# Norms inside the attention sweeps, cut in three: squares, then sums and root, then the scaling, each a unit later

## The reference, cut to what matters

```python
def rmsnorm(x, gain):
    xf = x.astype(jnp.float32)
    xf = xf * lax.rsqrt(jnp.mean(xf * xf, axis=-1, keepdims=True) + EPS)
    return xf.astype(x.dtype) * gain

def diff_mixer(q, k, v, qk_g, lam_p, o_g, lam_init):
    q = rmsnorm(q.reshape(B, S, DIFF_HEADS, 2, DIFF_QK), qk_g[0])
    k = rmsnorm(k.reshape(B, S, DIFF_HEADS, 2, DIFF_QK), qk_g[1])
    ...
    o = rmsnorm(o, o_g) * (1.0 - lam_init)

def swa_mixer(q, k, v, qk_g, sinks):
    q = rmsnorm(q.reshape(B, S, SWA_KV_HEADS, G, HEAD_DIM), qk_g[0])
    k = rmsnorm(k.reshape(B, S, SWA_KV_HEADS, HEAD_DIM), qk_g[1])
```

## Time and profile before

| | |
|---|---|
| median of 3 runs | 2279.16 us (2278.46 to 2280.85) |
| the profiled execution: its own time | 2280.71 us |
| its span in the profile | 2278.9 us |
| TensorE matmuls busy | 2146.6 us, 94% |
| VectorE busy | 1486.5 us, 65% |
| ScalarE busy | 1009.7 us, 44% |
| mean granted clock of TensorE | 0.983 |

### The profile page before, as it was taken

One profiled execution on the slowest core, in us unless ns is written; L12 is line 12 of the kernel. 1 busy time (PEld: TensorE's weight loads), 2 busy tenths in 40 slices (PEclk: granted clock), 3 DMA queues, 4 the chain that ended last, 5 costly groups with the idle time before them and its releaser, 6 DMA issues.

```text
span 2278.9 us, 32746 instructions
## 1 busy us (share of the span) xinstructions
PE 2146.6 (94%) x12051; PEld 1714.9 (75%) x12051; DVE 1486.5 (65%) x2695; ACT 1009.7 (44%) x1867; POOL 377.5 (17%) x346
## 2 busy tenths in 40 slices
PE   7999999999899998999999999999998989999996
PEld 4897788777677786777579878887866878777774
DVE  4637776654667876777656486766265678377775
ACT  4523334543465335555434233345344643345552
POOL 2002200000000341344300121000000014124441
PEclk9999999999999999999999999999999999999998
DMA  9322333331225675776542223423222266546753
GB/s 309 93 86 61 94 101 93 103 92 51 80 78 175 243 245 226 284 250 247 190 153 85 76 79 93 130 79 93 79 61 79 79 226 241 201 167 247 256 211 119
DMA packets 196573, 333.71 MB, mean 146 GB/s; under 512 B 30528, under 2 KB 153280, under 8 KB 180416
## 3 DMA queue, kind: packets, MB, share of 16 engines
q1 hardware_dynamic: 169184, 305.33, 39.6%
q0 software_dynamic: 19296, 19.98, 2.8%
q10 hardware_dynamic: 7936, 6.30, 0.8%
HBM read 352.48 MB, written 51.38 MB: 177 GB/s over the span
## 4 chain that ended last, share of the span: by engine, by line
PE 73%; DVE 13%; ACT 6%; issue 3%; DMA 3%; POOL 0%; SPq 0%; POOLq 0%; ACTq 0%; DVEq 0%
PE ps L874 68%; PE ps L872 5%; DVE spare L2077 2%; DVE ring_rounded L2095 2%; ACT WH_rounded L1587 2%; DVE nmax L2323 1%; DVE ssq L2262 1%; DMA SQKV<-gate_logits 1%; DMA DVt<-gate_logits 1%; DVE ps L2320 1%; DMA Y<-y_rows 1%; DVE DQK L2264 0%; DVE SC L2693 0%; ACT SC L1723 0%; POOL M L3035 0%
## 5 line engine op out<-in xcount | busy, mean ns | idle before, releaser
L874 PE MATMUL ps<-X_rounded,WH_rounded 128*128 128x512 f32 x768 | 343.8, 448 | 20.9 <-ACT CM L1635 6.5
L2095 DVE TENSOR_TENSOR ring_rounded<-ring,WH_rounded 128x512 fp32r<-128x512 f32 (+2 forms) x190 | 234.9, 1245 | 134.7 <-ACT WH_rounded L1587 134.3
L874 PE MATMUL ps<-H_rounded,WH_rounded 128*128 128x512 f32 x768 | 304.4, 396 | 8.9 <-DVE SC L2693 8.9
L874 PE MATMUL ps<-X_rounded,ring_rounded 128*128 128x512 f32 x768 | 304.3, 396 | 0.0
L874 PE MATMUL ps<-WH_rounded,X_rounded 128*128 128x256 f32 (+1 forms) x960 | 275.1, 287 | 3.1 <-ACT M L1868 1.0
L874 PE MATMUL ps<-ring_rounded,X_rounded 128*128 128x256 f32 (+1 forms) x960 | 271.5, 283 | 0.0
L874 PE MATMUL ps<-WH_rounded,H_rounded 128*128 128x256 f32 (+1 forms) x960 | 271.4, 283 | 0.0
L3035 POOL TENSOR_TENSOR M<-M,SC 128x512 f32<-128x512 f32 x48 | 75.8, 1591 | 997.9 <-DVE SC L2693 997.9
L1587 ACT ACTIVATE WH_rounded<-ring 128x512 fp32r<-128x512 f32 (+2 forms) x190 | 195.2, 1037 | 70.6 <-PE ps L874 62.3
L874 PEld LDWEIGHTS ps<-X_rounded,WH_rounded 128*128 128x128 f32 x768 | 146.7, 191 | 76.4 <-issue 30.4
L874 PEld LDWEIGHTS ps<-WH_rounded,X_rounded 128*128 128x128 f32 x960 | 184.8, 192 | 5.3 <-issue 2.4
(11 more groups left out here) (399 smaller groups left out, 4503.5 us busy)
## 6 DMA issues: line engine op xcount, KB each, us to landing
ring<-in_w_in SPq DMA_DIRECT2D x272, 256.0 KB, 3.9
Y<-in_moe_w_down SPq DMA_DIRECT2D x18, 1024.0 KB, 6.6
ring<-in_ada_w SPq DMA_DIRECT2D x64, 256.0 KB, 4.7
ring<-in_w_branch SPq DMA_DIRECT2D x64, 256.0 KB, 5.4
TM<-in_ada_w SPq DMA_DIRECT2D x14, 1024.0 KB, 10.2
DQK<-in_ada_w SPq DMA_DIRECT2D x14, 1024.0 KB, 9.4
ring<-in_moe_w_down SPq DMA_DIRECT2D x14, 1024.0 KB, 6.4
gate_logits<-CM SPq DMA_DIRECT2D x44, 256.0 KB, 2.9
```

The source lines that it names most:

```text
L874: ins = nc.tensor.matmul(o, lhsT, rhs, start=start, stop=stop)
L2095: ins = v.tensor_tensor(low[j][:, at:at + size], ring[:, j, at:at + size], high[i][:, at:at + size].bitcast(F32), ALU.subtract)
```

## The change

Inside the sweeps a norm is cut in three. ScalarE does only the squares at the end of unit n. In unit n+1 VectorE does the sums, after the combination and now ahead of the tile copy, and ScalarE the root, at the end of its unit, ahead of squares that a next norm may have there. In unit n+2 VectorE does the scaling and the gain, ahead of any sums and of the tile copy. Outside the sweeps the helper does the same as before, in the same order.

```diff
-            def head_norm(x, tmp, n, d):
+            def norm_squares(x, tmp):
                 act(tmp, x, ACT.Square).then_inc(squares_ready, p.gives(squares_ready))
+            def norm_root(n, d):
                 eng.wait_ge(sums_ready, p.next(sums_ready))
                 act(rsq[:, 0:n], ssq[:, 0:n], ACT.Ln, scale=1.0 / d, bias=consts[:, 0:1]).then_inc(
                     scalar_step, p.gives(scalar_step))
                 eng.wait_ge(scalar_step, p.given(scalar_step))
                 act(rsq[:, 0:n], rsq[:, 0:n], ACT.Exp, scale=-0.5).then_inc(rms_ready, p.gives(rms_ready))
+            def head_norm(x, tmp, n, d):
+                norm_squares(x, tmp)
+                norm_root(n, d)
...
                     for key, q in IN_SWEEP[s.kind].get(n, ()):
                         split_high(key, q)
+                    if n - 1 in NORM_IN_SWEEP[s.kind]:
+                        norm_root(*norm_of(*NORM_IN_SWEEP[s.kind][n - 1])[2:])
                     if n in NORM_IN_SWEEP[s.kind]:
                         step_, t = NORM_IN_SWEEP[s.kind][n]
                         if step_ == "dif_post":
                             eng.wait_ge(handed[t % 2], p.next(handed[t % 2]))
-                        head_norm(*norm_of(step_, t))
+                        norm_squares(*norm_of(step_, t)[:2])
...
-            def head_norm(x, tmp, n, d):
-                x = x if len(x.shape) == 3 else heads(x, n)
+            def norm_sums(tmp, n):
                 eng.wait_ge(squares_ready, p.next(squares_ready))
                 tmp = tmp if len(tmp.shape) == 3 else heads(tmp, n)
                 v.tensor_reduce(ssq[:, 0:n], tmp, AX, ALU.add).then_inc(sums_ready, p.gives(sums_ready))
+            def head_norm(x, tmp, n, d):
+                norm_sums(tmp, n)
+                norm_scale(x, n, d)
+            def norm_scale(x, n, d):
+                x = x if len(x.shape) == 3 else heads(x, n)
                 eng.wait_ge(rms_ready, p.next(rms_ready))
                 v.tensor_tensor(x, x, spread(rsq[:, 0:n], d), ALU.mult).then_inc(vector_step, p.gives(vector_step))
                 eng.wait_ge(vector_step, p.given(vector_step))
...
                     if s.kind == "diff" and 1 <= n <= s.units:
                         combine(n - 1)
+                    if n - 2 in NORM_IN_SWEEP[s.kind]:
+                        norm_in_sweep(*NORM_IN_SWEEP[s.kind][n - 2])
+                    if n - 1 in NORM_IN_SWEEP[s.kind]:
+                        norm_sums(*norm_of(*NORM_IN_SWEEP[s.kind][n - 1])[1:3])
                     if n >= 2 and s.last(n - 2):
                         tile_out(s, s.tile(n - 2))
-                    if n - 1 in NORM_IN_SWEEP[s.kind]:
-                        norm_in_sweep(*NORM_IN_SWEEP[s.kind][n - 1])
...
             def norm_in_sweep(step_, t):
-                head_norm(*norm_of(step_, t))
+                x, _, n, d = norm_of(step_, t)
+                norm_scale(x, n, d)
```

## The result

| | before | after |
|---|---|---|
| median | 2280.01 us (4 runs, 2278.46 to 2282.62) | 2248.15 us (4 runs, 2246.07 to 2253.79) |
| the profiled execution: own time | 2280.71 us | 2246.07 us |
| its span | 2278.9 us | 2244.3 us |
| mean granted clock of TensorE | 0.983 | 0.986 |

The ratio is 0.9859, with a 95% interval from 0.9841 to 0.9876: 32 us faster (28 to 36). The direction was right and the waits that went were the ones named; their size was not.

The account below looks back on a forecast made before the run. TensorE, with matmuls busy 94% of the span, was taken as the bound. Layer 0's 12.3 us and layer 1's 13.9 make 26.2 off 2280.71: 2254.5, by the median 2253, stated as 2254; range 2250 to 2267.

Parts of the forecast that it names:

- SWA: SWA sweep: waits of 0.57 and 0.74 us go, less 0.3 for a late row maximum: 1.0 us won.
- All four waits go: MLA sweep: TensorE's waits of 0.65, 0.31, 0.59 and 1.47 us at norms vanish, 3.0 us in layer 0.
- unit 4, with the clock behind it: Diff sweep: gate wait of 2.09 us goes and scores shorten, 2.2 us; clock recovered behind it gives 1.4.
- unit 5, scaling before the tile copy: Diff sweep: third SWA norm's scaling and gain delay the split TensorE waits for; 0.4 us given back.
- units 7 and 8: Diff sweep: 0.21 wait gone and a row maximum on time, +0.9; next row maximum 0.45 us late; net +0.4.
- unit 10: Diff sweep: wait of 0.33 us gone, +0.3 us; longer scores behind it not counted.
- unit 13, with the clock: Diff sweep: wait of 2.70 us before scores goes whole and 0.9 us of clock returns: +3.6 us.
- unit 16: Diff sweep: copy before the last values no longer stands behind the root: +0.8 us.
- (1): Rival: scaling delays row maxima, splits and combinations by 0.5 to 1 us; 12 us given back, 2266 us; chance 0.16.
- (2): Rival: remaining waits are followed by clock falls, or falls shift; 6 us lost, 2260 us; chance 0.13.
- (3): Rival: TensorE's next limits stand so close that under 4.6 us is won; 2276 us; chance 0.05.
- (4): Rival: VectorE becomes the bound of the sweeps; 6.5 us slower, 2286 us; chance 0.04.

Follow-up runs that it names:

- nearly empty norms: Against the changed kernel, squares, sums, scaling and gain of in-sweep norms cut to 16 columns or fewer, instructions and waits kept; 2243.19 us.
- the three further edits: Changed kernel plus combination ahead of split, scaling of diff units 3 and 6 norms later, gate copy ahead of exponentials in units 4 and 12; 2236.92 us.

## Why the prediction was right, and where its size was not

**The mechanism held.** All marks came as written: ScalarE's idle before the root under 5 us (0.5), the waits of 2.09, 2.70, 1.47, 0.65 and 0.59 gone, the clock full where it had been 0.52 and 0.64, the combination's wait at 1.20 for 1.15, with the second one of 1.17 that the sum had counted in. Only the split's wait grew less (1.31, not 1.5).

**Where the excess lies.** The sum was 26.2 us, the profiled executions differ by 34.6. Of the 8.4 us, MLA has 4.0 (10.0 against 6.0), diff 3.2 (21.4 against 8.3 + 9.9), SWA 2.1 (4.1 against 2.0) and the small stretches around them 1.1; the untouched stretch took 2.0 back. The largest is MLA's, and it is the one that a run of its own confirms. The range didn't cover it: its lower end of 2250 allowed for more clock, but took every wait at the same idle time.

**The step that failed: "All four waits go: 0.65 + 0.31 + 0.59 + 1.47 = 3.0 us" in MLA.** All four went, but were worth 5.0 us a layer (110.74 to 105.68, 109.67 to 104.74, with one fall of the clock in each of the four sweeps), and with the new order in MLA alone the medians give 13 us for both layers instead of 6. The idle time in a row is counted from the drawn end of the matmul before. The trace of before shows what that leaves out; here are TensorE's matmul ahead of the wait in the earlier trace rows and the weight load behind it:

```profile
461.78 0.39 PE L874 MATMUL ps<-X_rounded,ring_rounded 128*128 128x512 f32 x1
...
462.82 0.31 PEld L872 LDWEIGHTS ps<-ident,SC 128*128 128x128 f32 x3 [1.07 <-ACT SC L1723]
```

The matmul is drawn until 462.17, and 0.65 us later the turn begins. But matmuls of this shape start every 0.23 us, 0.16 before their drawn end: in the profile after the turn stands 0.23 behind its matmul (460.24, 460.47), in the one before 1.04. So this wait cost 0.81 by the starts of its two matmuls, and from the turn to the scores behind it 0.16 more (464.26 - 462.82 before, 461.75 - 460.47 after); from one unit's scores to the next it was 1.00. The same comparison gives 0.48 for the 0.31 and 0.89 for the 0.59. The last one shows it too: from one turn to the next it took 480.90 - 477.83 = 3.07 us before,

```profile
477.83 0.66 PE L872 MATMUL ps<-ident,SC 128*128 128x128 f32 x4
```

and 474.83 - 473.56 = 1.27 after, 1.80 for an idle time of 1.47. So the four waits were worth 4.2 us, not 3.0. The other 0.8 us are short waits that the sum had left out: one of the turn between units 25 and 26 cost 0.26 though its row shows no idle time at all, as it was shorter than the overlap, and at three more places 0.15 to 0.21 was lost. The weight loads' idle times (1.07, 0.55, 1.01 and 1.61 before the four, 4.2 together) were nearer. The Trainium skill, page "Perfetto Trace Analysis", section "Tensor Engine Instruction (MATMUL, LD_WEIGHTS)", says that the end of a matmul in a profile is estimated and not observed. The trace agrees as far as it can: the next matmul starts 0.16 us ahead of the drawn end.

**Diff, layer 0.** By the starts of the same matmuls, unit by unit:

| term | predicted | measured |
|---|---|---|
| unit 4, with the clock behind it | 2.2 + 1.4 | 4.0 |
| unit 5, scaling before the tile copy | -0.4 | -0.2 |
| units 7 and 8 | +0.4 | +0.7 |
| unit 10 | +0.3 | +0.4 |
| unit 13, with the clock | +3.6 | +3.6 |
| unit 16 | +0.8 | +1.0 |
| sum | 8.3 | 9.4 |

Every term has its sign and is within 0.4 us; most are a little small, probably for the same reason as in MLA.

**Layer 1 and the clock.** Diff won 12.0 us there, not 9.9. Two falls of before were missing from my account. One lies at the very start of layer 1's diff sweep, in front of the units (windows of before, the same stretch in layer 0 and in layer 1):

```profile
523.50:529.70 6.20, 5.52 (x41) 4.20 (x41) 2.84 (x4) 5.12 (x9) 0.00 (x0) 1.00 0.54 167
1645.90:1652.00 6.10, 5.81 (x36) 4.58 (x35) 2.37 (x2) 4.72 (x8) 0.00 (x0) 0.72 0.54 166
```

By the starts of the same matmuls it cost 0.9 us, which after doesn't have. With the 1.1 us by which layer 0 was above my figure too, that makes up the 2.1 us of excess but for 0.1; unit 13 won 1.6 us more than in layer 0, as forecast. The other lies in MLA: behind the 1.47 us wait that ends MLA the granted clock of before was full in layer 0 and not in layer 1, as its windows show:

```profile
480.00:491.00 11.00, 10.10 (x84) 10.03 (x85) 3.46 (x5) 4.43 (x7) 0.00 (x0) 1.00 0.46 120
1601.90:1613.00 11.10, 11.10 (x81) 11.02 (x81) 3.52 (x4) 3.41 (x5) 0.00 (x0) 0.85 0.44 120
```

11.1 x 0.15 = 1.7 us, lost in one layer and not in the other after the same wait; I had listed falls in the units of the diff sweep alone. After has no fall there, but one at the entry of the sweep that before has not (0.81 over 9 us), so in the length of layer 1's MLA the two about cancel.

**SWA.** 1.0 was predicted and 0.8 was won net in layer 0, by the starts of the matmuls behind the norm, but this agreement is luck: two errors cancel. The two waits were worth 1.95 us, not 0.57 + 0.74 = 1.31, and the row maximum behind the scaling gave back 1.1 us, not 0.3, in the two new waits of 0.33 and 0.32. The stage as a whole shows 2.4 and 1.7, but it also came out at 72.41 and 70.78 in the second profile of the same code, so the excess isn't the change's; in layer 0 it is a fall at the stage's end in before (granted clock 0.82 over the last 9.3 us, 1.00 after).

**The rivals.** (1), VectorE eats half, fell: nearly empty norms win only some 4 us more than full ones by the medians, whose intervals overlap, and 3 by the starts of the matmuls, where it had 12. (2), the clock stays low or falls elsewhere, fell in the sweeps; what stays of it is the entry of layer 1's MLA. (3), the waits change names, came in small: combination waits of 0.27 and 0.73 us stand where 0.12 and 0.18 had been and one of 1.17 where there was none, while others were there before (0.76, now 0.52; 1.15; the gate copy's 1.14). Old and new together, they left the 11 us that the three further edits took. (4) didn't happen, but two units instead of three went its way, 9 us slower, by another cause than it named: not too much work on VectorE, but a wait in front of it.

## What to carry to other kernels

When a step goes back and forth between two engines inside a paced loop, give each hand-over a whole turn of the loop, and check both directions: moving ScalarE's side and the sums but not the scaling turned a win of 33 us into a loss of 9, and moving VectorE's side alone left a win of 6. Size a TensorE wait by the starts of two matmuls against those of a like pair without the wait, or by the idle time of the weight load, not by the idle time drawn before a pipelined matmul: many short waits are under-counted most. Before comparing the lengths of a stage in two profiles, compare its granted clock. Once such waits are gone, the order of work within one engine's unit decides what the next wait is.

## What the hardware showed that I had not expected

- The clock falls after waits of the same length in one place and not in another: behind 1.47 us (3.07 from turn to turn) it stayed at 1.00 in layer 0 and was 0.85 over 11.1 us in layer 1.
- Where it falls differs between executions of one program. An untouched stretch of some 810 us took 805.74 us in one execution (granted clock 1.00) and 811.79 in another of the same code (0.99), and MLA sweeps of the same code took 103.39 to 106.30 us in one execution. The diff sweep of the changed kernel, which had no falls left, repeated to 0.04 us.
- Two profiled executions can differ by more than the medians: with the sums alone ahead of the tile copy the diff sweeps of the profile were 8 us shorter, some 6 of it clock, while the medians show 2.5 us (not told from none).
